# Probability maps of two attention stages: 32 x 32 squares on VectorE and a way through DRAM in place of transposes on TensorE

## What is computed

```python
# neighbourhood attention: 16 heads, 256 queries, 256 local keys and 256 context keys
s_loc = s_loc + bias[None]
s_ctx = jnp.einsum('brqhd,bchd->bhrqc', q, kc).astype(jnp.float32)
logits = jnp.concatenate([s_loc.reshape(...), s_ctx], axis=-1)
p = jax.nn.softmax(logits, axis=-1).astype(v.dtype)
o = jnp.einsum('bhrqik,brikhd->brqhd', p_blk, vb) + jnp.einsum('bhrqc,bchd->brqhd', p_ctx, vc)

# chunk attention: 8 heads, 256 queries, keys of this chunk and of those before it
s = jnp.einsum('bnqhd,bnkhd->bnhqk', qc, kb) * scale + bias
p = jax.nn.softmax(s, axis=-1)
o = jnp.einsum('bnhqk,bnkhd->bnqhd', p, vb)
```

## Time and profile before

| what | value |
|---|---|
| median of 3 runs | 1818.37 us (1818.0 to 1819.73) |
| span of the profiled execution | 1816.7 us |
| PE busy | 1797.5 us, 99% |
| POOL busy | 1365.0 us, 75% |
| DVE busy | 942.8 us, 52% |
| ACT busy | 905.1 us, 50% |

### The profile page before, as it was taken

The page is one execution under the profiler, slowest core; times in us unless marked ns, Lnnn a source line. Parts: engine busy times, 40 slices in busy tenths (PEclk is TensorE's granted clock), DMA queues, the critical chain, the costliest instruction groups (busy, mean ns, idle before and its releaser), DMA issues.

```text
span 1816.7 us, 25068 instructions
## 1 busy us (share of the span) xinstructions
PE 1797.5 (99%) x9322; PEld 1482.3 (82%) x9322; DVE 942.8 (52%) x1756; ACT 905.1 (50%) x1337; POOL 1365.0 (75%) x568
## 2 busy tenths in 40 slices
PE   6999999999999999999999999999999999999999
PEld 5888888887889888887888888888888878888887
DVE  4673766678655524776553230714095865143152
ACT  3334424764456644455554644464445565545442
POOL 2624544559868898987689798969897858888885
PEclk9999999999999999999999999999999999999999
DMA  9853885748775775565466566567655645656653
GB/s 366 299 201 93 278 301 164 196 157 301 245 279 188 221 216 194 172 209 165 132 187 195 175 195 195 193 184 232 195 195 181 186 139 163 194 160 211 190 194 128
DMA packets 200697, 366.61 MB, mean 202 GB/s; under 512 B 32868, under 2 KB 54356, under 8 KB 200020
## 3 DMA queue, kind: packets, MB, share of 16 engines
q1 hardware_dynamic: 197568, 357.39, 61.6%
q10 hardware_dynamic: 3028, 7.86, 1.1%
HBM read 364.12 MB, written 6.13 MB: 204 GB/s over the span
## 4 chain that ended last, share of the span: by engine, by line
PE 98%; DMA 0%; ACTq 0%; ACT 0%; DVE 0%; POOL 0%; issue 0%; DVEq 0%
PE ps L1258 26%; PE ps L1260 26%; PE ps L1259 26%; PE ps L1384 3%; PE ps L1385 3%; PE ps L1386 3%; PE ps L1949 1%; PE ps L1951 1%; PE ps L1950 1%; PE ps L1306 1%; PE ps L1876 1%; PE ps L1655 1%; PE ps L1626 1%; PE ps L1636 1%; PE ps L1516 1%; PE ps L1921 1%
## 5 line engine op out<-in xcount | busy, mean ns | idle before, releaser
L616 POOL TENSOR_TENSOR w_lo<-raw,w_hi 128x1024 fp32r<-128x1024 f32 x556 | 1346.0, 2458 | 403.4 <-ACT w_hi L654 382.2
L1258 PE MATMUL ps<-w_hi,act_rows_r 128*128 128x512 f32 x2064 | 814.8, 395 | 3.2 <-POOL w_lo L616 3.1
L1260 PE MATMUL ps<-w_hi,act_rows_r 128*128 128x512 f32 x2064 | 804.8, 390 | 0.0
L1259 PE MATMUL ps<-w_lo,act_rows_r 128*128 128x512 f32 x2064 | 804.5, 390 | 0.0
L654 ACT ACTIVATE w_hi<-raw 128x1024 fp32r<-128x1024 f32 x556 | 571.1, 1058 | 359.4 <-DMA raw<-in_ffn_w_up 96.5
L1258 PEld LDWEIGHTS ps<-w_hi,act_rows_r 128*128 128x128 f32 x2064 | 387.9, 188 | 89.9 <-issue 8.6
L1260 PEld LDWEIGHTS ps<-w_hi,act_rows_r 128*128 128x128 f32 x2064 | 387.8, 188 | 81.8
L1259 PEld LDWEIGHTS ps<-w_lo,act_rows_r 128*128 128x128 f32 x2064 | 388.1, 188 | 77.2
L2604 DVE STREAM_TRANSPOSE ps<-proj 32x256 f32<-32x256 f32 (+1 forms) x384 | 166.6, 434 | 6.5
L2585 DVE TENSOR_TENSOR proj<-proj,ps 128x1024 f32<-128x1024 f32 (+1 forms) x18 | 20.4, 1132 | 252.2 <-PE ps L1260 247.8
L1384 PE MATMUL ps<-act_rows_r,w_hi 128*128 128x512 f32 (+1 forms) x288 | 101.4, 352 | 0.0
(11 more groups left out here) (245 smaller groups left out, 1559.9 us busy)
## 6 DMA issues: line engine op xcount, KB each, us to landing
raw<-in_w_in SPq DMA_DIRECT2D x120, 512.0 KB, 3.8
raw<-in_ffn_w_gate SPq DMA_DIRECT2D x88, 512.0 KB, 4.3
raw<-in_ffn_w_up SPq DMA_DIRECT2D x88, 512.0 KB, 4.3
raw<-in_ffn_w_down SPq DMA_DIRECT2D x88, 512.0 KB, 3.4
proj<-in_ada_w SPq DMA_DIRECT2D x39, 512.0 KB, 7.8
pt<-in_ada_w SPq DMA_DIRECT2D x38, 512.0 KB, 6.4
raw<-in_pool_w_in SPq DMA_DIRECT2D x32, 512.0 KB, 7.4
raw<-in_na_w_in SPq DMA_DIRECT2D x32, 512.0 KB, 5.4
```

Of the source, the lines that this page charges most:

```text
L616: pool.tensor_tensor(w_lo[:, s, :], raw[:, s, :], w_hi[:, s, :].bitcast(F32), ALU.subtract).then_inc(lo_done, 1)
L1258: pe.matmul(o, h, hi, start=start, stop=False)
L1259: pe.matmul(o, h, lo, start=False, stop=False)
L1260: return pe.matmul(o, c, hi, start=False, stop=stop)
```

## The change

Six of the sixteen neighbourhood units (0, 2, 4, 6, 8, 10) and the four chunk units of each mix no longer use PE to turn their maps. DVE transposes each map in squares of 32 x 32 (one instruction of 1024 elements for each partition in the neighbourhood, of 768 in the mix). One DMA writes the result to DRAM, and four DMAs, one for each quarter of the partitions, read it back with the squares in their places. The product with the values then reads its moving operand in four pieces of 32 columns.

In the neighbourhood ACT issues these DMAs: the write of unit `u` in iteration `u + 3` (`keep_squares`), the four reads in iteration `u + 4` (`place_squares`), and PE makes the product in iteration `u + 5` in place of `u + 3`. The 512 KB buffer in DRAM, and that in SBUF, are single: the write of unit `u` waits until the reads of unit `u - 2` have landed, the reads wait for the write and for the product of `u - 2`. In the mix SP issues them between its weight loads (`keep_map`, `place_map`), with two buffers, and the product comes one unit later. ACT's and DVE's evictions of these transposes go. Unit 6's scaling and squares are moved behind the maxima of unit 7 (`MIX_DELAYED`). Some outputs move to another PSUM bank. The context half of the scores' copy and the new scores now wait for DVE's squares where they waited for the transposes.

```diff
+NA_SQUARED = (0, 2, 4, 6, 8, 10)
...
+MIX_B = 4
+
+MAP_KEPT, MAP_PLACED = {4: 25, 5: 27, 6: 31, 7: 32}, {4: 26, 5: 28, 6: 32, 7: 33}
+MIX_DELAYED = 6
...
+    map_rows = nc.dram_tensor("map_rows", (2, P, 768), F32, kind="Internal").ap()
+    na_squares = nc.dram_tensor("na_squares", (P, 1024), F32, kind="Internal").ap()
...
+            def keep_map(l, i):
+
+                sp.wait_ge(dve_done, dve_s.count(("map_t", l, i)))
+                if maps_before(l, i):
+                    sp.wait_ge(maps_in[i % 2], 64 * maps_before(l, i))
+                sp.dma_start(map_rows[i % 2], map_squares(i, [[1, 768]])).then_inc(maps_kept[i % 2], 16)
+
+            def place_map(l, i):
+
+                sp.wait_ge(maps_kept[i % 2], 16 * (maps_before(l, i) + 1))
+                sp.wait_ge(pe_done, pe_s.count(("ao", l, i - 2)))
+                for kq in range(4):
+                    src = bass.AP(map_rows.tensor, i % 2 * P * 768 + 192 * kq, [[768, 32], [32 * 768, 4], [1, 192]])
+                    sp.dma_start(map_turned(i, [[192, 4], [1, 192]], 0, slice(32 * kq, 32 * kq + 32)), src).then_inc(maps_in[i % 2], 16)
...
+                        if layer is not None:
+                            for i in range(MIX_B, MIX_SOFT):
+                                if g == SLOTS + MAP_PLACED[i]:
+                                    place_map(layer, i)
+                                if g == SLOTS + MAP_KEPT[i]:
+                                    keep_map(layer, i)
...
+                def keep_squares(u):
+
+                    act.wait_ge(dve_done, dve_s.count(("na_sq", u)))
+                    if u:
+                        act.wait_ge(na_placed, 64 * (u // 2))
+                    act.dma_start(na_squares[:], bias[:, 2048:3072]).then_inc(na_kept, 16)
+
+                def place_squares(u):
+
+                    act.wait_ge(na_kept, 16 * (u // 2 + 1))
+                    if u:
+                        act.wait_ge(pe_done, pe_s.count(("na_out", u - 2)))
+                    for kq in range(4):
+                        act.dma_start(na_placed_rows([[256, 4], [1, 256]], 0, slice(32 * kq, 32 * kq + 32)),
+                                      bass.AP(na_squares.tensor, 256 * kq, [[1024, 32], [32 * 1024, 4], [1, 256]])).then_inc(na_placed, 16)
...
+                    if i - 3 in NA_SQUARED:
+                        keep_squares(i - 3)
+                    if i - 4 in NA_SQUARED:
+                        place_squares(i - 4)
...
+                if u in NA_SQUARED:
+                    pe.wait_ge(na_placed, 64 * (u // 2 + 1))
...
-                        last = pe.matmul(ps[c * HD:(c + 1) * HD, bank, 0:P], v, pt[:, o:o + P], start=k == 0, stop=k == 3)
+                        maps = na_placed_rows([[256, 4], [1, 32]], 32 * (4 * c + k)) if u in NA_SQUARED else pt[:, o:o + P]
+                        last = pe.matmul(ps[c * HD:(c + 1) * HD, bank, 0:P], v, maps, start=k == 0, stop=k == 3)
...
+                    due = na_due(i)
+                    for u in due[:-1]:
+                        na_values(u)
...
-                    for c in range(1 if i < 4 else 2):
-                        read_out(6 + c)
-                        for k in range(3):
-                            last = pe.transpose(ps[:, 6 + c, k * P:(k + 1) * P], mix_rows_of(i, [[1, P]], c, k * P), ident[:])
-                        last.then_inc(pe_done, pe_s.one(("at", l, i, c)))
-                        held[6 + c] = ((dve_s if c else act_s), (f"apt{c}", l, i))
+                    read_out(6)
+                    for k in range(3):
+                        last = pe.transpose(ps[:, 6, k * P:(k + 1) * P], mix_rows_of(i, [[1, P]], 0, k * P), ident[:])
+                    last.then_inc(pe_done, pe_s.one(("at", l, i)))
+                    held[6] = (act_s, ("apt", l, i))
...
+                    elif i < MIX_SOFT:
+                        pe.wait_ge(maps_in[i % 2], 64 * (maps_before(l, i) + 1))
...
+                    if even and MIX_B <= i - 3 < MIX_SOFT:
+                        values(i - 3)
+                    if even and (0 <= i - 2 < MIX_B or MIX_SOFT <= i - 2 < MIX_UNITS):
                         values(i - 2)
-                    if not even and 1 <= i <= MIX_SOFT:
+                    if not even and 0 <= i - 1 < MIX_B:
...
+                    if u in NA_SQUARED:
+                        dve.wait_ge(act_done, act_s.count(("na_e", u, 1)))
+                        if u:
+                            dve.wait_ge(na_kept, 16 * (u // 2))
+                        dve.transpose(free(bias[:, 0:1], [[32, 8], [256, 4], [1, 32]], 2048),
+                                      na_rows_of(u, [[P, 8], [32, 4], [1, 32]])).then_inc(dve_done, dve_s.one(("na_sq", u)))
+                    else:
+                        dve.wait_ge(pe_done, pe_s.count(("na_t", u, 0)))
+                        if u >= 2:
+                            dve.wait_ge(pe_done, pe_s.count(("na_out", u - 2)))
+                        dve.tensor_copy(pt[:, (u % 2) * 1024:(u % 2) * 1024 + 512], ps[:, 6, :]).then_inc(dve_done, dve_s.one(("na_pt", u, 0)))
...
+                def squares_of_maps(i):
+
+                    dve.wait_ge(dve_done, dve_s.count(("aj", l, i)))
+                    if maps_before(l, i):
+                        dve.wait_ge(maps_kept[i % 2], 16 * maps_before(l, i))
+                    dve.transpose(map_squares(i, [[32, 6], [192, 4], [1, 32]]),
+                                  mix_rows_of(i, [[P, 6], [32, 4], [1, 32]])).then_inc(dve_done, dve_s.one(("map_t", l, i)))
...
+                        if i == MIX_DELAYED + 1:
+                            rows_scaled(MIX_DELAYED)
+                            squares_of_maps(MIX_DELAYED)
```

More of the change, by code:

```diff
@@ L230, in program @@
         decay_in = sem("decay_in")
+        na_kept, na_placed = sem("na_kept"), sem("na_placed")
+        maps_kept, maps_in = ([sem(f"{n}{k}") for k in range(2)] for n in ("maps_kept", "maps_in"))
         out_done = sem("out_done")
@@ L298, in na_out_bank, with na_due, na_last_of, na_placed_rows @@
         def na_out_bank(u):
-            return 2 if u < NA_UNITS - 3 else 4
+            return 3 if u == NA_SQUARED[-1] else 2 if u < NA_UNITS - 3 else 4
+        def na_due(i):
+            return [u for u in range(NA_UNITS - 1) if u + (5 if u in NA_SQUARED else 3) == i]
+        def na_last_of(k):
+            return 4 * k + 2 if 4 * k + 2 in NA_SQUARED else 4 * k + 3
+        def na_placed_rows(dims, at=0, rows=slice(0, P)):
+            return free(proj[rows, 0:1], dims, CTX_RES + D + at)
         def na_rows_of(u, dims, at=0):
@@ L307, in mix_rows_of, with map_squares, map_turned, maps_before @@
             return free(full[:, 0:1], dims, (i % 2) * 768 + c * 384 + at)
+        def map_squares(i, dims, at=0):
+            return free(proj[:, 0:1], dims, GATES + 1024 + (i % 2) * 768 + at)
+        def map_turned(i, dims, at=0, rows=slice(0, P)):
+            return free(pt[rows, 0:1], dims, (i % 2) * 768 + at)
+        def maps_before(l, i):
+            return 2 * l + (i - MIX_B) // 2
+        def mix_out_bank(i):
+            return {4: 6, 6: 6, 8: 6}.get(i, 7)
         def turn_bank(key, t, u):
@@ L919, in na_layer @@
                         u = i - 2
[L920 to L924, removed]
+                        if u not in NA_SQUARED:
+                            act.wait_ge(pe_done, pe_s.count(("na_t", u, 1)))
+                            if u >= 2:
+                                act.wait_ge(pe_done, pe_s.count(("na_out", u - 2)))
+                            act.activation(pt[:, (u % 2) * 1024 + 512:(u % 2) * 1024 + 1024], ps[:, 7, :],
+                                           ACT.Copy).then_inc(act_done, act_s.one(("na_pt", u, 1)))
                         if i == NA_UNITS:
@@ L1068, in probabilities @@
                 def probabilities(i):
[L1070 removed]
+                    act.wait_ge(pe_done, pe_s.count(("at", l, i)))
                     if i >= 2:
@@ L1073, in probabilities @@
                     act.activation(pt[:, (i % 2) * 768:(i % 2) * 768 + 384], ps[:, 6, 0:384],
-                                   ACT.Copy).then_inc(act_done, act_s.one(("apt0", l, i)))
+                                   ACT.Copy).then_inc(act_done, act_s.one(("apt", l, i)))
                 def y_square(i):
@@ L1732, in na_layer @@
                         turn_gate(1)
-                    if i >= 2:
+                    due = na_due(i)
+                    for u in due[:-1]:
+                        na_values(u)
+                    if i >= 2 and i - 2 not in NA_SQUARED:
                         na_turned(i - 2)
-                    if i >= 3:
-                        na_values(i - 3)
+                    for u in due[-1:]:
+                        na_values(u)
                     if i == NA_UNITS + 1:
@@ L2447, in na_layer @@
                         dve.wait_ge(pe_done, pe_s.count(("na_s", i)))
-                        if i >= 3:
+                        if i >= 3 and i - 3 not in NA_SQUARED:
```

(4 more changed lines are left out.)

87 lines of the change are left out of this document (39 added, 48 removed).

## The result

The changed kernel takes **1839.36 us** (median of 4 runs, 1837.39 to 1841.33) against 1818.51 (4 runs) of the kernel before on the same chip: a ratio of 1.011, 95% interval 1.010 to 1.0124. Forecast were 1815.8 us and a range up to 1827.0. It is slower, and the miss is 24 us.

A forecast was written before the change was run, and what follows sets the result against it. PE, busy 99% of the span, was taken as the bound. Span 1816.7 us, plus 2.7 for the neighbourhood, minus 5.3 for the mixes, gave 1814.1; with 1.7 from span to median, 1815.8 us, range 1807.5 to 1827.0.

The forecast's parts named there:

- What goes from PE: Neighbourhood and mixes: removed transposes save PE 5.8 us in each, 11.5 together, all of it showing.
- DVE and ACT at nothing: Both stages: DVE's squares (about 1.25 and 0.99 us) and ACT's five extra DMA issues were costed at nothing.
- The round trip: Neighbourhood: the single buffer's write-and-read loop of 9.15 us exceeds PE's 7.86 for two units; five periods idle PE 6.5 us.
- The bias, +1.5: Neighbourhood: bias loads behind the two DRAM-to-DRAM copies come late; could cost 3 us, taken as 1.5.
- The end of the loop, +0.5: Neighbourhood's end: outputs of units 10 and 12 cross and unit 12's evictions wait for the product of 10, 0.5 us.
- The first (the way hides): Neighbourhood: DRAM round trip of 8.05 us or less, PE idles at most 1 us, kernel takes 1808 us; chance 0.31.
- The second (DMA saturates): Neighbourhood: maps overload the DMA engines, writes, reads and bias loads land later, +4 to +6 us, 1822.5 to 1824.5; chance 0.28.
- The third (four pieces): Products with the values: reading the moving operand 32 columns at a time costs PE, 12.6 us if doubled, near 1828; chance 0.05.

The follow-up runs named there:

- e8: Changed kernel without the wait for unit 10 and with the two DRAM-to-DRAM copies issued among the neighbourhood stage's first weights: 1832.68 us.
- e12: Changed kernel with two places in DRAM and SBUF, products one iteration later, no wait for unit 10, copies behind the neighbourhood loop: 1817.2 us, ratio 0.9997.

## Where the prediction held and where it failed

- **What goes from PE.** Neighbourhood: held; a block of transposes is 0.97 us and the iteration without one is that much shorter. Mix: the term was 0.72 us a unit, priced with the neighbourhood's 0.12 us a transpose. In the mix the 24 of one layer take 2.37 us from start to start, 0.59 a unit (the block of the earlier trace rows at 864.61 ends where the next weight product begins). The new waits are 0.45 us a layer, not 0.25, and the retention product (L2009, L1921 before) takes 1.60 us for 1.50. 2.37 - 0.45 - 0.1 = 1.8 against 1.87 measured, and against 2.65 forecast.
- **DVE and ACT at nothing.** DVE's squares cost what was forecast, 1.24 and 0.98 us:

```profile
L2919 DVE STREAM_TRANSPOSE proj<-full 128x768 f32<-128x768 f32 x8 | 7.8, 978 | 0.3
...
L2491 DVE STREAM_TRANSPOSE bias<-full 128x1024 f32<-128x1024 f32 x4 | 5.0, 1238 | 4.8 <-DMA na_squares<-bias 4.8
```

  As compute they were hidden. The waits that stand beside them on these engines were not: ACT's ahead of the reads, part of its idle 8.57 us, and DVE's of 4.76 ahead of the next squares. The cover that I took for ACT's issues held in part: ahead of the split behind the reads it was idle 0.4 to 1.8 us at four other units. That this reached PE is not shown.
- **The round trip, the step that failed most.** The term was 5 x 1.29 = 6.5 us, from a loop of 9.15 us with landings of 3.6 and 3.3 us, and PE waited 18.6 us for maps. The mechanism was the one forecast: one place, and a write that waits for the reads before it. Its size was wrong. Three of the five loops took 9.0, 9.8 and 8.7 us, but the two beside a copy of 1280 KB took 18.3 and 15.5: the write and the reads of unit 2 landed after 9.8 and 5.7, the reads of unit 4 after 9.5. I had the copies' 8.7 us in a row and charged them to the bias alone. With the copies away (e8) the loops were still 8.5 to 12.2 us, and PE waited 9.6 for maps. The Trainium skill ("DMA: Bandwidth & Descriptors", Issuing engines are not separate DMA queues) says that DMAs of all issuers interleave on the same engines, and this trace agrees: ACT's write took 9.8 us with SP's copy under way, against a median of 3.4 with the copies away. The same page (Anatomy of one DMA) has a fixed price of 2.0 us plus bytes over 436 GB/s, which makes an estimate of 3.2 us for the write; the medians of this stage were 4.7, and 3.4 with the copies away. A second thing was missing: even without copies the way of unit 2 took 12.2 us from write to product, against 8 of PE between. The forecast compared a loop with a pair of iterations and never the way of one map with the time until its product.
- **The bias, +1.5.** Right in kind, too small in size. In the run without the way it is 4.4 us of PE's wait at one unit, hidden in the changed kernel by the longer waits for maps.
- **The end of the loop, +0.5.** The mechanism was named as it is (the evictions of unit 12 wait for the product of 10) and priced at a tenth: 4.3 us by the times, 5.0 without the way. DVE waited 6.37 us for it in the changed kernel, and everything behind it on DVE too.
- **The clock** stood in no term, and no reason was given for that. It cost some 7 us, an estimate from the stretches above.
- **Rivals.** The first (the way hides) is refuted: with the mended order it still isn't hidden for nothing. The second (DMA saturates) had the right sign and place, but at 4 to 6 us its price was a fourth of the loss of 21, since it spread the load evenly instead of asking what a single copy does to a single write. The third (four pieces) is refuted by 1.09 us for sixteen products.

Adding up from the changed kernel's stage to that of e12: false wait 2.4, second place 5.7, one iteration more 4.5, copies 8.0, together 20.6 of the 23.4 us. What is left, 2.8 with 4.8 saved, is the waits above: 4.9 us at the scores, 1.9 for maps, and 0.8 in no single row. That those at the scores come from the chain of scores, ACT's copy, DVE's sum and the banks' release, which is no shorter though PE's iteration is, is argued from the rows and was not tested. The two places in the load order that looked idle cost the kernel before 7 to 9 us by loads behind the copies in SP's queue: the pooling weights (ACT's row above), and at the early place the bias loads, which took SP 15.8 us to issue instead of 11.4, so that the loads of `in_ada_w` behind them came 4 us later. Why the issues took longer is open.

## What to carry to other kernels

Price a way through DRAM by its latency in the busiest place it meets (here 12 us, and 18 beside one 1280 KB copy on another queue), and compare it with the work between the write and the use, not with the loop's period alone. When data moves to another buffer, go through every wait that guarded the old one: a wait that was free becomes a stall when the order around it changes. A saving on the engine that bounds the kernel is worth only what the next chain in the loop lets through; try it on half the units first.

## What the runs showed of the hardware that I had not expected

- A 512 KB write on ACT's queue took 9.8 us beside a 1280 KB DRAM-to-DRAM copy that SP had issued 0.9 us ahead, against a median of 3.4 in the run with the copies away.
- After PE stood for 10.3 and 5.7 us, its granted clock was 0.50 and a unit's sixteen products took 1.98 us instead of 1.09; the level lasted 3.9 and 5.6 us into the work. In e12, with no wait over 1.6 us, it was 1.00 throughout the stage.
- Transposes are not one price: 0.12 us each in the neighbourhood, 0.10 in the mix.
- The same two copies left the kernel before without a wait of PE in the neighbourhood's loop and the same time behind it, but cost it 7.4 us at the first weights of that stage, and 8.9 us ahead of the next pooling stage.
